# Attention softmax in whole-tile operations: subtraction and row sum on VectorE, one exponential a chunk on ScalarE

## The chip, the cores and the metric

The kernel runs on one core of a Trainium2 chip. A core has five engines that work side by side and are ordered by semaphores: TensorE (PE, matrix products into PSUM), VectorE (DVE), ScalarE (ACT), GpSimd (POOL) and SyncE (SP, which here only starts transfers). Each engine works through its own instructions in order. The metric is the device time of one execution in microseconds; the time given is the median of several executions.

## The reference

One layer of a hybrid encoder over 1024 frames of 1024 channels, float32. A projection feeds three token mixers (gated DeltaNet, RWKV-7, sliding-window attention with sinks), whose outputs are gated, summed, projected and normalised; a feed-forward part follows. The change is in the attention branch. Frames come in 16 chunks of 64; a chunk's 64 queries read the 128 keys of the chunk before and their own, for 8 heads. What is computed there:

```python
s = einsum(qc, kb) * SD ** -0.5 - slope * dist      # [8 heads, 64 queries, 128 keys] a chunk
s = where(key_chunk >= 0, s, -inf)
p = softmax(concatenate([s, sink], -1), axis=-1)[..., :-1]
o = einsum(p, vb)
```

The sink is one learned logit per head that takes part in the maximum and in the sum, and has no value of its own.

## The kernel before, in words

The program is a row of stages, each with its own block of instructions for every engine: the projection and the preparation of operands; `scan_and_attend` (L1054), which runs both recurrences over the 16 chunks and does the attention in between; `mix_and_project`; `feed_forward`. A stage starts when the one before has ended on all engines, its last stores included. The change is in `scan_and_attend` alone.

The order of the work there is written out by hand. Each engine has three generators for a chunk: `product(c)` (products of a chunk's operands that don't need the state), `state(c)` (what needs the recurrent state and updates it) and `attend(c)`. `run` (L1110) takes their parts in turn by the list `TURNS`: in the loop of chunk c these are `state(c)`, `product(c + 1)` and `attend(c)`. Every engine follows the same list, so that one engine's queue fixes what stands behind a waiting instruction.

The attention of a chunk holds its 8 x 64 rows of scores as one tile `score[b]` of 128 partitions x (4 x 128) columns, two tiles in turn. Four numbers belong to each partition: `top` (maximum), `own` (the sink's part) and `rest` (the sum), tiles of 128x4. PE computes the scores (L1278). On DVE follow the scaling with the ALiBi penalty (L1364), the row maximum (L1366), the maximum with the sink (L1368), sink minus maximum (L1370) and the maximum's sign turned (L1371). ACT takes the exponential of `own` (L1431) and four exponentials of 128x128, each with the negative maximum as bias and the row sum as accumulated output (L1433). In a later turn DVE adds the sink's part to the sum (L1374), takes the reciprocal (L1376) and multiplies the tile by it (L1378). PE transposes the weights (L1285), ACT copies them out of PSUM (L1437), PE multiplies them with the values (L1293), ACT copies the result out (L1442).

In DVE's order around this: after the maximum's part come `state`'s sums of the new state, L1339 (waits for PE's L1243), L1342 (`s_g`) and L1349 (`sv`), then `product`'s L1323 (`zt`), then L1374 to L1378; the next chunk's L1329 and L1333 (`r_tmp`, `r_g`), L1313, L1316, L1318 follow, and then L1364 again. In ACT's order L1433 is followed by L1420 (waits for PE's L1204) and L1411 (waits for PE's L1264). POOL, once DVE has finished `s_g`, scales it (L1482, `s_dec`), copies inverse blocks (two L1466, four L1470) and scales `tok_g` (L1473), then waits for the next `s_g`; it runs one chunk ahead, so that its copies end before the last two chunks.

Of the kernel before, what the change touches and what calls it, by code (L numbers as in the profile page):

```python
# [18 lines left out]
ALU = mybir.AluOpType  # L19
ACT = mybir.ActivationFunctionType  # L20
AX = mybir.AxisListType

P = 128
# [97 lines left out]
class Phase(ExitStack):  # L121
# [7 lines left out]
    def sem(self, name):  # L129
        self.sems.append(self.held.enter_context(self.nc.semaphore(name)))  # L130
        return self.sems[-1]
# [918 lines left out]
def rwkv_rows(e):  # L1050
    return slice(64 * e, 64 * e + 64)


def scan_and_attend(nc, home, opnd, xinv, gates_tile, cols, egl_bc, plast, mixed, u, attended, par, tab, const_dram):  # L1054
# [8 lines left out]
    with Phase(nc, home) as local:  # L1063
# [20 lines left out]
        W = 2 * C  # L1084
        keys, values = (local.enter_context(nc.sbuf_tensor(n, shape, F32)) for n, shape in (("at_keys", [P, SKV, C + T]), ("at_values", [P, C + T])))
        alibi = local.enter_context(nc.sbuf_tensor("at_alibi", [P, 8 * W], F32))
        score, weight, vt = two("at_score", [4, W]), local.enter_context(nc.sbuf_tensor("at_weight", [P, 4, W], F32)), two("at_vt", [P])
        top, own, rest = two("at_top", [4]), two("at_own", [4]), two("at_rest", [4])
# [11 lines left out]
        mm_sc, mm_t, mm_pv, vt_done, scored, topped, exp_done, rested, p_done, weight_done, at_done = (  # L1100
            sem("at_" + n) for n in ("mm_sc", "mm_t", "mm_pv", "vt_done", "scored", "topped", "exp_done", "rested", "p_done", "weight_done", "done"))
# [8 lines left out]
        def run(product, state, attend):  # L1110


            first = product(0)
            for _ in range(4):
                next(first, None)
            for c in range(NCH):
                parts = {"state": state(c), "product": product(c + 1) if c + 1 < NCH else iter(()), "attend": attend(c)}
                for part in TURNS:
                    next(parts[part], None)
# [182 lines left out]
        @block.vector  # L1302
        def _(dve):
            for e in range(2):
                dve.memset(sv[0][rwkv_rows(e), of(e), :], 0.0).then_inc(s_rw_done, 1)
            dve.memset(s_g[0][:, :, :], 0.0).then_inc(s_g_done, 2)

            def product(c):
                b, d = c % 2, c % DEEP
                dve.wait_ge(mm_m, c + 1)  # L1310
                for e in range(2):
                    other = rwkv_rows(1 - e)
                    dve.tensor_tensor(ar[d][other, of(e), 0, :], ps_m[e][other, :, 0, :], bc("strict", 4, other), ALU.mult).then_inc(masked, 1)  # L1313
                yield
                for e in range(2):
                    dve.tensor_tensor(causal[b][:, of(e), :], ps_m[e][:, :, 1, :], bc("causal", 4), ALU.mult).then_inc(masked, 1)  # L1316
                dve.wait_ge(mm_a, c + 1)
                dve.tensor_tensor(attn[b][:, :, :], ps_a[:, 0:2, :],  # L1318
                                  gates_tile[:, c:c + 1, :, 1, :].rearrange("p o g s -> p (o g) s"), ALU.mult).then_inc(attn_done, 1)
                yield  # L1320
                dve.wait_ge(mm_z, c + 1)
                dve.wait_ge(inv_done, c * 4 + 4)
                dve.tensor_tensor(zt[b][:, :, :], ps_z, inv[b][:, 1, :, :], ALU.add).then_inc(zt_done, 1)  # L1323
                yield

            def state(c):
                b, d = c % 2, c % DEEP
                dve.wait_ge(mm_r, c + 1)
                dve.tensor_tensor(r_tmp[b][:, :, :], ps_r[:, 256:512].rearrange("p (g d) -> p g d", g=2),  # L1329
                                  cols[:, c:c + 1, 2, :].rearrange("p o g -> p (o g)").unsqueeze(2).to_broadcast([P, 2, GD]), ALU.mult).then_inc(r_tmp_done, 1)  # L1330
                dve.wait_ge(r_tmp_done, c + 1)
                dve.wait_ge(tok_done, c + 1)
                dve.tensor_tensor(r_g[b][:, :, :], r_tmp[b][:, :, :], tok_g[b][:, 1, :, :], ALU.add).then_inc(r_g_done, 1)  # L1333
                yield
                yield
                dve.wait_ge(mm_s, c + 1)
                for e in range(2):
                    h = rwkv_rows(e)
                    dve.tensor_tensor(s_sum[b][h, :, :], sv[d][h, of(e), :], ps_r[h, 0:256].rearrange("p (j d) -> p j d", j=4), ALU.add).then_inc(s_sum_done, 1)  # L1339
                dve.wait_ge(dec_done, c + 1)  # L1340
                for e, src in enumerate((ps_w[:, 0:256], ps_r[:, 256:512])):
                    last = dve.tensor_tensor(s_g[1 - b][:, :, :].rearrange("p (g e) d -> p g e d", e=2)[:, :, e, :],  # L1342
                                             s_dec[b][:, :, :].rearrange("p (g e) d -> p g e d", e=2)[:, :, e, :],
                                             src.rearrange("p (g d) -> p g d", g=2), ALU.add)
                    last.then_inc(s_g_done, 1)
                dve.wait_ge(s_sum_done, c * 2 + 2)
                for e in range(2):
                    h = rwkv_rows(e)
                    dve.tensor_tensor(sv[(c + 1) % DEEP][h, of(e), :], s_sum[b][h, :, :],  # L1349
                                      plast[h, :].rearrange("p (j c) -> p j c", j=4)[:, :, c:c + 1].to_broadcast([64, 4, C]), ALU.mult).then_inc(s_rw_done, 1)  # L1350
                yield

            def attend(c):
                b = c % 2
                at = 4 * W if c == 0 else 0
                flat = lambda x: x.rearrange("p j k -> p (j k)")
                yield
                yield
                if c == 0:
                    dve.wait_ge(alibi_landed, 16)  # L1360
                dve.wait_ge(mm_sc, c + 1)
                if c >= 2:
                    dve.wait_ge(mm_t, c - 1)
                dve.scalar_tensor_tensor(flat(score[b][:, :, :]), ps_at[:, :], SD ** -0.5, alibi[:, at:at + 4 * W], ALU.mult, ALU.add).then_inc(scored, 1)  # L1364
                dve.wait_ge(scored, c + 1)
                dve.tensor_reduce(top[b][:, :], score[b][:, :, :], AX.X, ALU.max).then_inc(topped, 1)  # L1366
                dve.wait_ge(topped, 4 * c + 1)
                dve.tensor_tensor(top[b][:, :], top[b][:, :], par("sinks", 0, 4), ALU.max).then_inc(topped, 1)  # L1368
                dve.wait_ge(topped, 4 * c + 2)
                dve.tensor_tensor(own[b][:, :], par("sinks", 0, 4), top[b][:, :], ALU.subtract).then_inc(topped, 1)  # L1370
                dve.tensor_scalar(top[b][:, :], top[b][:, :], -1.0, None, ALU.mult).then_inc(topped, 1)  # L1371
                yield
                dve.wait_ge(exp_done, 5 * c + 5)
                dve.tensor_tensor(rest[b][:, :], rest[b][:, :], own[b][:, :], ALU.add).then_inc(rested, 1)  # L1374
                dve.wait_ge(rested, 2 * c + 1)
                dve.reciprocal(rest[b][:, :], rest[b][:, :]).then_inc(rested, 1)  # L1376
                dve.wait_ge(rested, 2 * c + 2)
                dve.tensor_tensor(score[b][:, :, :], score[b][:, :, :], rest[b][:, :].unsqueeze(2).to_broadcast([P, 4, W]), ALU.mult).then_inc(p_done, 1)  # L1378
                yield
                yield  # L1380

            run(product, state, attend)

        @block.scalar
        def _(act):
# [38 lines left out]
            def attend(c):  # L1424
                b = c % 2
                if c:
                    store_attended(c - 1)
                yield
                yield
                act.wait_ge(topped, 4 * c + 4)  # L1430
                act.activation(own[b][:, :], own[b][:, :], ACT.Exp).then_inc(exp_done, 1)  # L1431
                for j in range(4):
                    act.activation(score[b][:, j, :], score[b][:, j, :], ACT.Exp, bias=top[b][:, j:j + 1], accum_out=rest[b][:, j:j + 1]).then_inc(exp_done, 1)  # L1433
                yield
                yield
                act.wait_ge(mm_t, c + 1)
                act.activation(weight[:, :, :], at_t, ACT.Copy).then_inc(weight_done, 1)  # L1437
                yield

            def store_attended(c):  # L1440
                act.wait_ge(mm_pv, c + 1)
                act.activation(attended[:, :, c * C:(c + 1) * C], ps_at[:, 0:4 * C].rearrange("p (j s) -> p j s", j=4), ACT.Copy).then_inc(at_done, 1)  # L1442

            run(product, state, attend)
            store_attended(NCH - 1)
            finish(NCH - 1)
# [804 lines left out]
```

## Time and profile before

| | us |
|---|---|
| median of 3 runs | 2146.53 (2145.28 to 2147.59) |
| the profiled execution's own time | 2144.27 |
| its span, first to last instruction | 2142.4 |
| PE busy in the span | 1976.5 (92%) |
| DVE busy | 1100.6 (51%) |
| ACT busy | 581.8 (27%) |
| POOL busy | 564.3 (26%) |

The busy shares are means over all stages. The stage of the change is the stretch from about 855 to 1076 us. Busy times of several engines overlap. A row of a timeline gives start and duration in us, then engine, line, operation and tiles; in brackets stands how long the engine had been idle before and what it waited for.

### The profile page before, as it was taken

To read this page: it belongs to the slowest core of one execution; us is meant where nothing else is said; L and a number is where in the kernel's file an instruction comes from. 1 tells how busy PE (TensorE), PEld (TensorE's weight loads), DVE (VectorE), ACT (ScalarE), POOL (GpSimd) and SP (SyncE) were. 2 spreads that over 40 slices of the span, in tenths; PEclk is the share of its full clock that TensorE was granted. 3 is DMA by queue.
4 is the path that set the end of the run, shared out by engine and by line. 5 is a ranking of instruction groups with operands and counts; after the bars stand their busy time and mean duration, and the time that the engine had idled before them with its cause. 6 is when DMAs were issued, how large, how long until landed. Compare 5 with 4: busy or idle time off the path is not lost. (4 is left out here: it accounts for less than half of the span.)

```text
span 2142.4 us, 28824 instructions
## 1 busy us (share of the span) xinstructions
PE 1976.5 (92%) x11456; PEld 1575.0 (74%) x11456; DVE 1100.6 (51%) x1351; ACT 581.8 (27%) x926; POOL 564.3 (26%) x357
## 2 busy tenths in 40 slices
PE   5998889999999997999888899599999999999995
PEld 4876668767788885777666678488888888888884
DVE  3666764566449600666668744522433434424337
ACT  2443423235321211444442221212212112121112
POOL 3211111211122322434242372422212122122113
PEclk9999989999999998999999999799999999999998
DMA  5243565135753554666364460211111111111101
GB/s 141 52 80 93 130 153 147 40 89 134 177 148 97 127 124 127 188 187 193 90 187 144 135 207 20 59 60 59 49 39 59 29 59 59 29 59 44 44 20 79
DMA packets 340405, 211.83 MB, mean 99 GB/s; under 512 B 170796, under 2 KB 310700, under 8 KB 338256
## 3 DMA queue, kind: packets, MB, share of 16 engines
q1 hardware_dynamic: 264112, 156.33, 27.4%
q10 hardware_dynamic: 75568, 54.04, 8.8%
q8 instruction: 71, 1.16, 0.2%
q0 software_dynamic: 624, 0.05, 0.1%
q14 instruction: 30, 0.25, 0.0%
HBM read 151.27 MB, written 59.06 MB: 98 GB/s over the span
## 5 line engine op out<-in xcount | busy, mean ns | idle before, releaser
L154 PE MATMUL bank<-xhi,w_hi 128*128 128x512 f32 x976 | 396.3, 406 | 2.9 <-DVE xlo L868 2.9
L155 PE MATMUL bank<-xlo,w_hi 128*128 128x512 f32 x976 | 387.8, 397 | 0.0
L156 PE MATMUL bank<-xhi,w_lo 128*128 128x512 f32 x976 | 387.1, 397 | 0.0
L394 POOL TENSOR_TENSOR w_lo<-w_raw,w_hi 128x1024 fp32r<-128x1024 f32 x61 | 163.0, 2673 | 640.5 <-ACT w_hi L731 640.5
L2139 DVE TENSOR_TENSOR ff_hid<-ff_hid,ff_ps_u 128x512 f32<-128x512 f32 x42 | 28.9, 687 | 416.8 <-PE ff_ps_u L156 416.8
L154 PEld LDWEIGHTS bank<-xhi,w_hi 128*128 128x128 f32 x976 | 185.0, 190 | 49.1 <-issue 3.5
L156 PEld LDWEIGHTS bank<-xhi,w_lo 128*128 128x128 f32 x976 | 184.7, 189 | 44.9
L155 PEld LDWEIGHTS bank<-xlo,w_hi 128*128 128x128 f32 x976 | 184.9, 189 | 44.7 <-issue 2.4
L2147 DVE TENSOR_TENSOR y<-y,ff_d 128x512 f32<-128x512 f32 x320 | 199.0, 682 | 0.0
L2050 POOL TENSOR_TENSOR ff_lo_down<-ff_raw_down,ff_hi_down 128x1024 fp32r<-128x1024 f32 x22 | 52.9, 2405 | 533.0 <-ACT ff_hi_down L1987 533.0
L154 PE MATMUL ff_ps_g<-x1hi,ff_hi_gate 128*128 128x512 f32 x352 | 137.8, 391 | 18.2 <-POOL ff_lo_gate L2050 18.2
L154 PE MATMUL ff_d<-ff_hi_down,ff_hhi 128*128 128x512 f32 x352 | 139.8, 397 | 4.8 <-DVE ff_hlo L2156 3.9
L155 PE MATMUL ff_d<-ff_lo_down,ff_hhi 128*128 128x512 f32 x352 | 138.1, 392 | 0.0
L156 PE MATMUL ff_d<-ff_hi_down,ff_hlo 128*128 128x512 f32 x352 | 138.1, 392 | 0.0
L155 PE MATMUL ff_ps_g<-x1lo,ff_hi_gate 128*128 128x512 f32 x352 | 137.4, 390 | 0.0
L156 PE MATMUL ff_ps_g<-x1hi,ff_lo_gate 128*128 128x512 f32 x352 | 137.4, 390 | 0.0
L154 PE MATMUL ff_ps_u<-x1hi,ff_hi_up 128*128 128x512 f32 x352 | 136.9, 389 | 0.0
L155 PE MATMUL ff_ps_u<-x1lo,ff_hi_up 128*128 128x512 f32 x352 | 136.9, 389 | 0.0
L156 PE MATMUL ff_ps_u<-x1hi,ff_lo_up 128*128 128x512 f32 x352 | 136.9, 389 | 0.0
L717 ACT ACTIVATE work<-bank 128x512 f32<-128x512 f32 x70 | 41.9, 598 | 274.5 <-PE bank L156 269.4
L154 PEld LDWEIGHTS ff_ps_g<-x1hi,ff_hi_gate 128*128 128x128 f32 x352 | 66.5, 189 | 32.4 <-POOL ff_lo_gate L2050 18.6
L154 PEld LDWEIGHTS ff_d<-ff_hi_down,ff_hhi 128*128 128x128 f32 x352 | 66.5, 189 | 27.7 <-DVE y L2147 9.4
(320 smaller groups left out, 3527.4 us busy)
## 6 DMA issues: line engine op xcount, KB each, us to landing
w_raw<-in_w_in ACTq DMA_DIRECT2D x61, 512.0 KB, 4.2
op<-opnd SPq DMA_DIRECT2D x16, 1152.0 KB, 5.6
u<-work ACTq DMA_DIRECT2D x68, 256.0 KB, 3.4
b_gate<-u SPq DMA_DIRECT2D x24, 512.0 KB, 3.8
ff_raw_gate<-in_ffn_gate SPq DMA_DIRECT2D x22, 512.0 KB, 4.0
ff_raw_up<-in_ffn_up SPq DMA_DIRECT2D x22, 512.0 KB, 5.3
ff_raw_down<-in_ffn_down SPq DMA_DIRECT2D x22, 512.0 KB, 5.8
opnd<-work SPq DMA_DIRECT2D x20, 512.0 KB, 6.2
```

What stands on the lines that cost most here:

```text
L154: pe.matmul(out, w_hi, x_hi, start=first, stop=False)
L155: pe.matmul(out, w_hi, x_lo, start=False, stop=False)
L156: return pe.matmul(out, w_lo, x_hi, start=False, stop=last)
L394: pool.tensor_tensor(w_lo[b][:, :, :], w_raw[b][:, :, :], as_f32(w_hi[b][:, :, :]), ALU.subtract).then_inc(w_lo_done, 1)
L717: act.activation(to, bank[(done_at[q] - 1) % 3][:, :], form(tile)).then_inc(evac, 1)
L2050: pool.tensor_tensor(wlo[b][n][:, :, :], raw[b][n][:, :, :], as_f32(whi[b][n][:, :, :]), ALU.subtract).then_inc(lo_done, 1)
L2139: dve.tensor_tensor(hid[:, h, :], hid[:, h, :], ps_u[:, h, :], ALU.mult).then_inc(mul_done, 1)
L2147: dve.tensor_tensor(part, part, ps_d[n % 4][:, :], ALU.add).then_inc(added, 1)
```

## The change

Before the exponential DVE subtracts the maximum from the whole 128x512 tile, with the maximum broadcast along each row, in place of turning the maximum's sign. ACT takes one exponential over the tile, without a bias and without the accumulated sums, in place of four. After it DVE sums the rows with a reduction over the tile, in front of the addition of the sink's part. The semaphore counts follow: two signals a chunk from ACT in place of five, three steps in place of two for `rested`. The maximum's part still signals `topped` four times.

```diff
--- before.py
+++ after.py
@@ -1368,13 +1368,15 @@
                 dve.tensor_tensor(top[b][:, :], top[b][:, :], par("sinks", 0, 4), ALU.max).then_inc(topped, 1)
                 dve.wait_ge(topped, 4 * c + 2)
                 dve.tensor_tensor(own[b][:, :], par("sinks", 0, 4), top[b][:, :], ALU.subtract).then_inc(topped, 1)
-                dve.tensor_scalar(top[b][:, :], top[b][:, :], -1.0, None, ALU.mult).then_inc(topped, 1)
-                yield
-                dve.wait_ge(exp_done, 5 * c + 5)
+                dve.tensor_tensor(score[b][:, :, :], score[b][:, :, :], top[b][:, :].unsqueeze(2).to_broadcast([P, 4, W]), ALU.subtract).then_inc(topped, 1)
+                yield
+                dve.wait_ge(exp_done, 2 * c + 2)
+                dve.tensor_reduce(rest[b][:, :], score[b][:, :, :], AX.X, ALU.add).then_inc(rested, 1)
+                dve.wait_ge(rested, 3 * c + 1)
                 dve.tensor_tensor(rest[b][:, :], rest[b][:, :], own[b][:, :], ALU.add).then_inc(rested, 1)
-                dve.wait_ge(rested, 2 * c + 1)
+                dve.wait_ge(rested, 3 * c + 2)
                 dve.reciprocal(rest[b][:, :], rest[b][:, :]).then_inc(rested, 1)
-                dve.wait_ge(rested, 2 * c + 2)
+                dve.wait_ge(rested, 3 * c + 3)
                 dve.tensor_tensor(score[b][:, :, :], score[b][:, :, :], rest[b][:, :].unsqueeze(2).to_broadcast([P, 4, W]), ALU.mult).then_inc(p_done, 1)
                 yield
                 yield
@@ -1429,8 +1431,7 @@
                 yield
                 act.wait_ge(topped, 4 * c + 4)
                 act.activation(own[b][:, :], own[b][:, :], ACT.Exp).then_inc(exp_done, 1)
-                for j in range(4):
-                    act.activation(score[b][:, j, :], score[b][:, j, :], ACT.Exp, bias=top[b][:, j:j + 1], accum_out=rest[b][:, j:j + 1]).then_inc(exp_done, 1)
+                act.activation(score[b][:, :, :], score[b][:, :, :], ACT.Exp).then_inc(exp_done, 1)
                 yield
                 yield
                 act.wait_ge(mm_t, c + 1)
```

## Rows read from the trace of the kernel before

**Rows 1.** Stretch, length; busy us (count) of PE, PEld, DVE, ACT, POOL; clock; DMA.

```profile
945.00:958.15 13.15, 12.48 (x224) 9.94 (x224) 9.13 (x23) 5.52 (x21) 5.19 (x8) 1.00 0.59 171
...
1050.00:1063.00 13.00, 10.48 (x186) 8.14 (x184) 7.66 (x20) 5.70 (x21) 1.09 (x1) 1.00 0.08 24
```

**Rows 2.** Waits from 868 to 1063 us: us in total, times, longest.

```profile
DVE s_sum L1339 <- PE ps_r L1243: 21.2, 15, 1.6
...
PE ps_at L1285 <- DVE at_score L1378: 6.9, 14, 0.7
```

**Rows 3.** Timeline of DVE around chunk 6: start us, us, line, tiles.

```profile
944.97 0.87 DVE L1339 TENSOR_TENSOR s_sum<-sv,ps_r 64x256 f32<-64x256 f32 x2 [1.40 <-PE ps_r L1243]
...
946.53 1.60 DVE L1349 TENSOR_TENSOR sv<-s_sum,plast 64x256 f32<-64x256 f32 x2
...
946.97 1.16 DVE L1349 TENSOR_TENSOR sv<-s_sum,plast 64x256 f32<-64x256 f32 x1
...
948.17 0.56 DVE L1323 TENSOR_TENSOR zt<-ps_yz,inv 128x384 f32<-128x384 f32 x1
...
948.64 0.15 DVE L1374 TENSOR_TENSOR at_rest<-at_rest,at_own 128x4 f32<-128x4 f32 x1
...
949.04 0.80 DVE L1378 TENSOR_TENSOR at_score<-at_score,at_rest 128x512 f32<-128x512 f32 x1
...
955.55 0.69 DVE L1366 TENSOR_REDUCE at_top<-at_score 128x4 f32<-128x512 f32 x1
...
956.55 0.16 DVE L1371 TENSOR_SCALAR at_top<-at_top 128x4 f32<-128x4 f32 x1
...
958.11 0.87 DVE L1339 TENSOR_TENSOR s_sum<-sv,ps_r 64x256 f32<-64x256 f32 x2 [1.40 <-PE ps_r L1243]
```

**Rows 4.** Timeline of ACT in the same chunk.

```profile
956.98 0.27 ACT L1393 ACTIVATE at_vt<-ps_yz 128x128 f32<-128x128 f32 x1
...
957.23 0.40 ACT L1433 ACTIVATE at_score<-at_score,at_top 128x128 f32<-128x128 f32 x1
...
958.77 0.37 ACT L1420 ACTIVATE o<-ps_a 128x256 f32<-128x256 f32 x1
...
962.61 0.38 ACT L1411 ACTIVATE o_tok<-ps_o 128x256 f32<-128x256 f32 x1 [3.47 <-PE ps_o L1264]
```

**Rows 5.** Timeline of PE in the same chunk.

```profile
949.90 0.66 PE L1285 MATMUL ps_at<-tables,at_score 128*128 128x128 f32 x4 [0.48 <-DVE at_score L1378]
...
957.99 0.44 PE L1204 MATMUL ps_a<-tables,o_tok 128*128 128x128 f32 x2
```

**Rows 6.** Timeline of POOL in the same chunk.

```profile
946.76 1.09 POOL L1482 TENSOR_TENSOR s_dec<-s_g,egl_bc 128x512 f32<-128x512 f32 x1 [7.45 <-DVE s_g L1342]
...
948.80 0.50 POOL L1470 COPY inv<-inv_packed 32x384 f32<-32x384 f32 x1
...
949.36 0.85 POOL L1470 COPY inv<-inv_packed 32x384 f32<-32x384 f32 x1
```

**Rows 7.** Timeline of DVE and POOL in chunk 7.

```profile
959.68 0.86 DVE L1349 TENSOR_TENSOR sv<-s_sum,plast 64x256 f32<-64x256 f32 x2
...
961.05 0.42 DVE L1374 TENSOR_TENSOR at_rest<-at_rest,at_own 128x4 f32<-128x4 f32 x1
...
961.72 0.75 DVE L1378 TENSOR_TENSOR at_score<-at_score,at_rest 128x512 f32<-128x512 f32 x1
...
960.19 1.26 POOL L1482 TENSOR_TENSOR s_dec<-s_g,egl_bc 128x512 f32<-128x512 f32 x1 [7.74 <-DVE s_g L1342]
...
961.59 0.33 POOL L1466 COPY join<-inv_corner 32x192 f32<-32x192 f32 x1
```

**Rows 8.** Timeline of DVE and PE in chunk 15, the last.

```profile
1064.96 0.69 DVE L1378 TENSOR_TENSOR at_score<-at_score,at_rest 128x512 f32<-128x512 f32 x1
...
1065.77 0.66 PE L1285 MATMUL ps_at<-tables,at_score 128*128 128x128 f32 x4
```

**Rows 9.** Line L1437: durations ns min/median/max, first and last start, form.

```profile
L1437 ACT ACTIVATE at_weight<-ps_at x16: 597/597/597, 871.7 to 1066.5; 128x512 f32<-128x512 f32 x16
```

## The prediction

> **What bounds the kernel now.** The change touches only the stage that scans the chunks and attends, so I read the stretch from about 855 to 1076 us and took the rest as it is. First the busy times of one ordinary chunk [rows 1]: PE works 12.48 of 13.15 us at a granted clock of 1.00, DVE 9.13, ACT 5.52, POOL 5.19. PE works through its instructions in order, so the question is what its few gaps wait for. The table of waits [rows 2] answers it: PE stands before the transposes of the weights (L1285) in 14 chunks, 6.9 us in all, for DVE's last multiplication (L1378). DVE in its turn waits 21.2 us over 15 chunks for the products behind L1243. That closes the loop that makes the chunk's length. The timeline of chunk 6, counted from 0, shows it: DVE starts L1339 at 944.97, runs without a pause up to the end of L1378 at 949.84, PE starts L1285 at 949.90, and PE's work from there leads to L1339 of the next chunk at 958.11 [rows 3, 5]. 4.93 us of DVE and handover plus 8.21 us led by PE make the period of 13.14. Whatever makes DVE's run from L1339 to L1378 longer makes every chunk longer. Work elsewhere costs nothing while its cover lasts.
>
> **The maximum's half of the change** (before the exponential). The 128x4 multiplication by -1 (0.16 us) goes, and a 128x512 subtraction with a broadcast operand comes. It has the shape of L1378: 0.69 us alone, 0.80 beside POOL [rows 3, 8]. It starts at 956.55, where POOL stands idle (7.74 us before its s_dec in chunk 7) [rows 7], so I take 0.69 and end at 957.24. DVE then waits anyway until 958.11, 1.40 us behind the present last instruction [rows 3]. The cost of 0.53 (0.64 with the contended duration) is hidden, and 0.87 of cover remain. It counts only if that wait vanishes.
>
> **ScalarE.** Four exponentials with their accumulator reads now run from 957.23 to 958.77, 1.54 us [rows 4]. One over 128x512 replaces them. The nearest row is the 0.60 us copy of that size from PSUM [rows 9]; even the bounds, one 128-wide exponential (0.40) and the present 1.54, lead to the same answer. It waits for the subtraction, so the small exponential in front starts at about 957.3 instead of 957.14 and the large one ends near 958.0. Behind it in ACT's queue stands L1420, which needs PE's L1204, ended at 958.43, so it starts 0.3 us sooner and ACT then idles 3.8 us instead of 3.47 for L1411 [rows 4, 5]. DVE's first reader of the sums starts at 961.05 [rows 7], 3 us after that end (2.3 after the present one). ScalarE's saving of some 0.9 us a chunk is therefore worth nothing.
> The Trainium skill, "VectorE: DVE Perf Modes", section on the TRN2 errata, gives ScalarE a fixed extra latency per instruction that large tiles amortise, which argues for this merge. The trace agrees on the size (0.40 for 128 columns, 0.60 for 512); summed at face value over 16 chunks it would promise 15 us, of which I count none, since no wait of rows 2 ends on ACT's exponential.
>
> **The sum's half** (after the exponential). A reduction of 128x512 comes before the small addition. The same form takes 0.69 us at L1366, with 0.036 to the next dependent instruction [rows 3]: +0.72, all of it inside DVE's run to L1378. Nothing covers it. This is the first term.
>
> **The second term is POOL.** The added reduction moves the last three operations to another place beside POOL's copies, and the rows show that the two engines take turns. The second L1349 starts at 946.97 and should take 0.41; it takes 1.16 and ends 0.28 after POOL's s_dec has ended (946.76 + 1.09 = 947.85). L1378 starts at 949.04 in the first inv copy, which ends at 949.30, and ends 0.54 after it. The second copy, started at 949.36, takes 0.85 in place of 0.50 and ends 0.37 after L1378. In chunk 7 even the 4-column L1374 takes 0.42 and ends with s_dec at 961.47 [rows 3, 6, 7]. L1323 and L1339, with one operand in PSUM, do not show it. So a DVE instruction with two SBUF inputs stands until a POOL instruction that got in first has ended, and the other way round.
> New order: the reduction, one input, runs from 948.64 to about 949.33; the first copy is over at 949.30; the addition starts at 949.35 or 949.36, together with the second copy at 949.36. Who gets in first? A stopped instruction has its beginning behind it by then: the second copy 0.13 us (its 0.50 less the 0.37 that followed L1378), a DVE instruction 0.13 (L1349: 0.41 less 0.28) to 0.15 (L1378: 0.69 less 0.54). By this the copy gets in at 949.49 and the addition between 949.48 and 949.51. I choose the copy, knowing that it is close.
> Then the addition ends 0.02 behind the copy, at 949.88. The multiplication starts 0.25 later, as now (948.79 to 949.04, with the reciprocal between), at 950.13, inside the third copy (949.92 to 950.42), and ends 0.54 behind that, at 950.96, where it was 949.84: +1.12 a chunk. If the addition gets in first, it ends at 949.51, and the multiplication starts at 949.76, finds the second copy just over and ends at 950.45: +0.61, counted as 0.62.
> The Trainium skill, "SBUF — State Buffer", section "Who interferes with whom", says that GpSimd and a VectorE instruction with two SBUF inputs contend, that whoever issues first keeps the shared ports for the whole instruction, and that a reduction never contends. The rows agree (1.16 for 0.41; L1366 is always 0.69, though POOL is idle beside it, so the reduction's part is not shown here).
>
> **Sum.** POOL copies run in chunks 0 to 13. In chunk 14 POOL has one instruction left, s_dec (1.09 us from 1050 to 1063) [rows 1], so it pays 0.72. In chunk 15 PE starts L1285 at 1065.77 without a wait on DVE, 0.12 behind the end of L1378 at 1065.65, where 0.06 is the usual handover (949.84 to 949.90), so 0.66 of the 0.72 arrive [rows 3, 5, 8]. 14 x 1.12 + 0.72 + 0.66 = 17.1 us. The next stage begins behind this one's last stores, so the shift is passed on. The profiled execution took 2144.27 us (span 2142.4), so 2161.4 in its terms; the median of the runs shown is 2.3 above it, and 2146.5 + 17.1 gives 2163.6. I write 2163.5.
>
> **Rivals.**
> A. The addition gets in first. 14 x 0.62 + 0.72 + 0.66 = 10.1 us, 2156.6. For it: the margin is as small as the rounding of the rows. Against it: the order worked out above.
> B. Not slower. In chunk 7, POOL's s_dec starts 0.51 us after the first L1349 (959.68, 960.19) instead of 0.23 (946.53, 946.76), so that the second L1349 gets in first and the pair takes 0.86 in place of 1.60; that chunk's run from L1339 (958.11) to the end of L1378 (962.47) is 4.36 instead of 4.87 [rows 3, 6, 7]. If the new timing gave every chunk this order, then: reduction 961.05 to 961.73, addition behind the first join copy (961.59 + 0.33) to 961.96, multiplication (started at 962.21) behind the second (961.98 to 962.33) to 962.87, so 4.76: 0.11 below today's ordinary chunk. 13 x -0.11, chunk 7 itself +0.40, and 1.38 for the last two give +0.4: 2146.9, no change. It decides when s_dec starts more than about 0.2 us later than it does in 14 of 15 chunks. Against it: the change touches nothing between s_g and s_dec.
> C. ScalarE's saving lies on the path. Even then a chunk has -0.94 + 0.53 + 0.72 = +0.31, 5 us over 16 chunks: 2151.5. Against it: the 3 us between its end and its reader.
> D. The reduction is held up by POOL as well, or holds up a copy into which the addition then runs: up to one copy's remainder, some 0.35 us a chunk on top of the forecast, 14 x 0.35 = 5: 2168.5.
> The clock is not among them: in the chunk with the largest gaps PE worked 10.48 of 13 us and was still granted 1.00 [rows 1], and the new chunk has 12.5 of 14.3.
>
> **How the numbers follow.** Forecast 0.50, A 0.33, B 0.08, C 0.03, D 0.04, something else with a gain 0.02. The range reaches from A with its error of the median (2154.5) to short of D (2167). Between no change and either sign this kernel's runs tell 0.2%, 4.3 us. Forecast, A, C and D are slower: 0.90. B is no change: 0.08. Faster: 0.02.
>
> **What would show it.** Right: the period of an ordinary chunk goes from 13.15 to about 14.27 us; the small addition takes about 0.5 instead of 0.15; PE's wait before L1285 grows from 0.48 to 1.6; DVE's wait at L1339 falls from 1.40 to about 0.9; ACT's wait before L1411 grows to 3.8; the new exponential takes about 0.6. With A, the addition takes 0.15 and the period is 13.77. With B the pair at L1349 takes 0.86 in most chunks. Wrong altogether: a period that stays, or a wait before L1285 that ends on ACT; also a granted clock below 1.00 inside the stage, which would make it slower than the range.

## The result and the profile after

| | before | changed |
|---|---|---|
| median, us | 2145.91 (2143.68 to 2147.59, 4 runs) | 2158.38 (2154.70 to 2158.89, 4 runs) |
| profiled execution, us | 2144.27 | 2154.70 |
| its span, us | 2142.4 | 2152.9 |
| period of an ordinary chunk, us | 13.15 | 13.75 |

The changed kernel is slower by a factor of 1.0055, 95% interval 1.0038 to 1.0072; 12.5 us between the medians, 10.4 us between the two profiled executions. The direction and the range were right. The forecast case (+1.12 us a chunk) was not the one that came: rival A did, in which VectorE's small addition gets in ahead of POOL's second copy.

DVE of the changed kernel in chunk 6, the answer to [rows 3]. L1371 is now the subtraction, L1374 the added reduction, L1376 the addition, L1380 the multiplication:

```profile
948.70 0.68 DVE L1371 TENSOR_TENSOR at_score<-at_score,at_top 128x512 f32<-128x512 f32 x1
950.26 0.87 DVE L1339 TENSOR_TENSOR s_sum<-sv,ps_r 64x256 f32<-64x256 f32 x2 [0.88 <-PE ps_r L1243]
...
951.83 1.60 DVE L1349 TENSOR_TENSOR sv<-s_sum,plast 64x256 f32<-64x256 f32 x2
953.46 0.56 DVE L1323 TENSOR_TENSOR zt<-ps_yz,inv 128x384 f32<-128x384 f32 x1
953.93 0.68 DVE L1374 TENSOR_REDUCE at_rest<-at_score 128x4 f32<-128x512 f32 x1
954.64 0.16 DVE L1376 TENSOR_TENSOR at_rest<-at_rest,at_own 128x4 f32<-128x4 f32 x1
954.84 0.18 DVE L1378 RECIPROCAL at_rest<-at_rest 128x4 f32<-128x4 f32 x1
955.05 0.69 DVE L1380 TENSOR_TENSOR at_score<-at_score,at_rest 128x512 f32<-128x512 f32 x1
...
964.01 0.87 DVE L1339 TENSOR_TENSOR s_sum<-sv,ps_r 64x256 f32<-64x256 f32 x2 [0.88 <-PE ps_r L1243]
```

The run from L1339 to the end of the multiplication is 950.26 to 955.74, 5.48 us, where it was 4.87. The reduction brings 0.71 with its handover, and the multiplication gives 0.11 back, 0.69 for 0.80 (the sum, 0.60, and the 0.61 of the runs differ by rounding). From one L1339 to the next it is 13.75. In the maximum's half the subtraction (0.68) takes its time out of DVE's wait, 0.88 instead of 1.40.

ACT and PE in the same chunk, the answer to [rows 4, 5]:

```profile
949.52 0.61 ACT L1434 ACTIVATE at_score<-at_score 128x512 f32<-128x512 f32 x1
950.61 0.38 ACT L1422 ACTIVATE o<-ps_a 128x256 f32<-128x256 f32 x1 [0.48 <-PE ps_a L1204]
...
954.75 0.38 ACT L1413 ACTIVATE o_tok<-ps_o 128x256 f32<-128x256 f32 x1 [3.75 <-PE ps_o L1264]
```

```profile
955.80 0.66 PE L1285 MATMUL ps_at<-tables,at_score 128*128 128x128 f32 x4 [1.09 <-DVE at_score L1380]
```

The one exponential takes 0.61 us where four took 1.54. Of the 0.93 us saved, ACT waits 0.76: 0.48 in front of L1422, where it had no wait, and 3.75 in front of L1413 for 3.47. The rest goes in front of its exponentials, which start later behind the subtraction. PE's wait before the transposes is 1.09 for 0.48; that 0.61 is the loss of a chunk.

POOL's copies beside them, the answer to [rows 6]:

```profile
954.09 0.50 POOL L1471 COPY inv<-inv_packed 32x384 f32<-32x384 f32 x1
...
954.64 0.54 POOL L1471 COPY inv<-inv_packed 32x384 f32<-32x384 f32 x1
...
955.24 0.87 POOL L1471 COPY inv<-inv_packed 32x384 f32<-32x384 f32 x1
```

The addition and the second copy start at the same printed 954.64. The addition keeps its 0.16 and the copy takes 0.54, so the addition went first. The first copy runs beside the reduction and keeps its 0.50, and the reduction keeps its 0.68: a reduction, with one input, does not take turns with POOL here. The prediction had no row for it; this is one. The Trainium skill, "SBUF — State Buffer", section "Who interferes with whom", says the same, that a reduction never contends with GpSimd.

The first and the last L1339 of both profiles tell how much of the 10.4 us is the stage's (durations in ns, then first and last start in us). Kernel before, then changed kernel:

```profile
L1339 DVE TENSOR_TENSOR s_sum<-sv,ps_r x32: 411/420/426, 866.1 to 1062.5; 64x256 f32<-64x256 f32 x32
```

```profile
L1339 DVE TENSOR_TENSOR s_sum<-sv,ps_r x32: 411/419/426, 867.7 to 1073.2; 64x256 f32<-64x256 f32 x32
```

Before, the distance is 196.4 us, after 205.5, which is +9.0 before rounding, and +0.65 behind it up to the start of the next stage (1071.17 and 1082.49 for its first ACT instruction). That is 9.7 us of the stage: 13 chunks of 0.61, chunk 7 with 0.41, chunk 14 with 0.72, and the end. The changed kernel's stage began 1.7 us later, which is the execution and not the change, and the later stages took 0.8 us less. The difference of the medians, 12.5, has the same noise in it.

### The profile page after: what moved, and what is told of

Read it like the earlier page. It is cut to its first block and busy times, and to the rows that moved or that the text cites. A ratio compares the mean times of both kernels' runs of the same rounds, so it can differ in the third digit from the quotient of the medians.

```text
span 2152.9 us, 28728 instructions
## 1 busy us (share of the span) xinstructions
PE 1979.3 (92%) x11456; PEld 1576.7 (73%) x11456; DVE 1116.5 (52%) x1367; ACT 568.5 (26%) x814; POOL 564.8 (26%) x357
## 3 DMA queue, kind: packets, MB, share of 16 engines
q8 instruction: 71, 1.16, 0.2%
```

## The experiments

The theory, called P in the expectations, is that of the prediction: only VectorE's run from L1339 to the multiplication sets the length of a chunk, and in that run VectorE takes turns with POOL. Q and S let every VectorE or ScalarE microsecond count. The experiments ran in two sets, each on one chip together with the kernel before: x1 to x4 (its median there 2146.76 over 23 runs) and x5 to x8 (2146.17 over 17). Every ratio is to the kernel before of the same set.

**x1_max_half.** The subtraction alone.

```diff
-                dve.tensor_scalar(top[b][:, :], top[b][:, :], -1.0, None, ALU.mult).then_inc(topped, 1)
+                dve.tensor_tensor(score[b][:, :, :], score[b][:, :, :], top[b][:, :].unsqueeze(2).to_broadcast([P, 4, W]), ALU.subtract).then_inc(topped, 1)
...
-                    act.activation(score[b][:, j, :], score[b][:, j, :], ACT.Exp, bias=top[b][:, j:j + 1], accum_out=rest[b][:, j:j + 1]).then_inc(exp_done, 1)
+                    act.activation(score[b][:, j, :], score[b][:, j, :], ACT.Exp, accum_out=rest[b][:, j:j + 1]).then_inc(exp_done, 1)
```

> Only the maximum's half: VectorE subtracts the maximum from the tile (L1371 as in the changed kernel), ScalarE keeps four exponentials with accumulated sums, without a bias; nothing is added after them. Theory P (only VectorE's run from L1339 to the last multiplication sets the chunk): time as before within 2 us, period of a chunk 13.15, VectorE's wait at L1339 falls from 1.40 to about 0.88. Theory Q (each added VectorE microsecond counts): 16 x 0.53 = 8.5 us slower.

Measured: 2145.55 us, ratio 0.9997 (0.9984 to 1.0010).

```profile
943.03 0.68 DVE L1371 TENSOR_TENSOR at_score<-at_score,at_top 128x512 f32<-128x512 f32 x1
944.59 0.87 DVE L1339 TENSOR_TENSOR s_sum<-sv,ps_r 64x256 f32<-64x256 f32 x2 [0.88 <-PE ps_r L1243]
...
948.67 0.80 DVE L1378 TENSOR_TENSOR at_score<-at_score,at_rest 128x512 f32<-128x512 f32 x1
...
957.74 0.87 DVE L1339 TENSOR_TENSOR s_sum<-sv,ps_r 64x256 f32<-64x256 f32 x2 [0.88 <-PE ps_r L1243]
```

The period is 13.15 as before (once 13.29) and the wait 0.88. The subtraction is free; Q's 8.5 us lie outside the interval.

**x2_sum_half.** The reduction alone: four exponentials with bias, without `accum_out`, and the changed kernel's reduction with its counts.

```diff
-                    act.activation(score[b][:, j, :], score[b][:, j, :], ACT.Exp, bias=top[b][:, j:j + 1], accum_out=rest[b][:, j:j + 1]).then_inc(exp_done, 1)
+                    act.activation(score[b][:, j, :], score[b][:, j, :], ACT.Exp, bias=top[b][:, j:j + 1]).then_inc(exp_done, 1)
...
+                dve.tensor_reduce(rest[b][:, :], score[b][:, :, :], AX.X, ALU.add).then_inc(rested, 1)
```

> Only the sum's half: ScalarE takes four exponentials with the bias but without the accumulated sums, VectorE reduces the tile before the small addition. Theory P: as slow as the changed kernel, 10 us over the kernel before, period 13.75 (+0.61), last multiplication 0.69 instead of 0.80, PE's wait before the transposes 1.09. Theory Q: less than the changed kernel by the subtraction's 8.5 us, so about 4 us over before.

Measured: 2158.77 us, ratio 1.0054 (1.0036 to 1.0073). The whole loss of the change is here. Its trace shows more: the small addition took 0.16 us in most chunks, and 0.51 in four. Two neighbours, chunks 5 and 6: DVE, then PE's wait, then POOL's second copy of each:

```profile
944.60 0.16 DVE L1376 TENSOR_TENSOR at_rest<-at_rest,at_own 128x4 f32<-128x4 f32 x1
...
958.35 0.51 DVE L1376 TENSOR_TENSOR at_rest<-at_rest,at_own 128x4 f32<-128x4 f32 x1
...
959.10 0.84 DVE L1380 TENSOR_TENSOR at_score<-at_score,at_rest 128x512 f32<-128x512 f32 x1
```

```profile
945.75 0.66 PE L1285 MATMUL ps_at<-tables,at_score 128*128 128x128 f32 x4 [1.09 <-DVE at_score L1380]
...
960.00 0.66 PE L1285 MATMUL ps_at<-tables,at_score 128*128 128x128 f32 x4 [1.59 <-DVE at_score L1380]
```

```profile
944.59 0.53 POOL L1472 COPY inv<-inv_packed 32x384 f32<-32x384 f32 x1
...
958.34 0.50 POOL L1472 COPY inv<-inv_packed 32x384 f32<-32x384 f32 x1
```

Both times the copy starts 0.01 us before the addition; once the addition passes (the copy takes 0.53), once it stands (0.51) and the multiplication then stands behind the third copy (0.84). The forecast case and rival A occur side by side in one execution, and PE's wait is then 1.59, the forecast's 1.6. The trace holds whole nanoseconds, and these part the cases: in the nine chunks where the addition passed it had started 0 to 4 ns after the copy, in the four where it stood 5 or 6 ns after it. In the changed kernel's profile it lies between 1 ns before and 4 ns after, and always passes.

From the first to the last L1339 x2 takes 210.7 us in its profile, 5.2 more than the changed kernel: 4 x 0.50 for these chunks and two periods that are longer by 1.6 us each (see x7). The medians (2158.77 and 2158.38) are nearly equal all the same. Whether the changed kernel has such chunks in its other executions, which lie 3.5 to 4.2 us above the profiled one, no trace shows.

**x3_one_exp.** ScalarE's merge alone.

```diff
-                for j in range(4):
-                    act.activation(score[b][:, j, :], score[b][:, j, :], ACT.Exp, bias=top[b][:, j:j + 1], accum_out=rest[b][:, j:j + 1]).then_inc(exp_done, 1)
+                act.activation(score[b][:, :, :], score[b][:, :, :], ACT.Exp).then_inc(exp_done, 1)
```

The kernel leaves out the subtraction of the maximum and the row sums: `rest` is filled with ones at the start (two lines more, so that later line numbers of DVE are higher by 2), and DVE waits for two signals of ACT in place of five.

> Only ScalarE's merge: one exponential over the tile in place of four; the maximum is not subtracted and the row sums are not formed (left out), VectorE's instructions are those of the kernel before. Theory P: no change within 2 us although ScalarE has about 0.9 us a chunk less to do; ScalarE's wait for PE's L1264 grows by that. Theory S (ScalarE's time counts): up to 15 us faster.

Measured: 2145.47 us, ratio 0.9995 (0.9983 to 1.0007); periods of 13.15 again (once 13.33). ScalarE's waits before L1420 and L1411 (L1422 and L1413 here) take up what it saves, 0.60 and 0.28 us of the 0.91:

```profile
948.33 0.63 ACT L1434 ACTIVATE at_score<-at_score 128x512 f32<-128x512 f32 x1
949.56 0.38 ACT L1422 ACTIVATE o<-ps_a 128x256 f32<-128x256 f32 x1 [0.60 <-PE ps_a L1204]
...
953.70 0.38 ACT L1413 ACTIVATE o_tok<-ps_o 128x256 f32<-128x256 f32 x1 [3.75 <-PE ps_o L1264]
```

The merge brings nothing here, in either direction. The profiled execution, 2149.97 us, is above that median: in its last chunk PE ran at a granted clock of 0.50 (same columns as in [rows 1]), where the kernel before had 1.00:

```profile
1067.00:1075.00 8.00, 7.31 (x57) 4.56 (x56) 2.74 (x8) 1.44 (x5) 0.00 (x0) 0.50 0.09 33
```

**x4_later.** The changed kernel with the run's last four instructions pushed back a little.

```diff
+                dve.tensor_reduce(top[b][:, 0:1], top[b][:, :], AX.X, ALU.max)
                 dve.tensor_reduce(rest[b][:, :], score[b][:, :, :], AX.X, ALU.add).then_inc(rested, 1)
```

> The changed kernel with one more reduction over 4 columns (result not used) in front of the row sum, so that the row sum, the addition, the reciprocal and the multiplication move by about 0.08 us against POOL. Theory P with turn taking between VectorE and POOL: the small addition now meets POOL's second inv copy after that copy has got in, takes about 0.5 instead of 0.16, and the multiplication stands behind the third copy; period about 14.3 instead of 13.75, some 7 us slower than the changed kernel. Rival, no such edge (the place beside the copies doesn't matter): period 13.83, 1.3 us slower.

Measured: 2170.03 us, ratio 1.0102 (1.0078 to 1.0126), 11.65 us above the changed kernel's median, more than either expectation.

```profile
936.16 0.15 DVE L1374 TENSOR_REDUCE at_top<-at_top 128x1 f32<-128x4 f32 x1
936.23 0.68 DVE L1375 TENSOR_REDUCE at_rest<-at_score 128x4 f32<-128x512 f32 x1
936.94 0.45 DVE L1377 TENSOR_TENSOR at_rest<-at_rest,at_own 128x4 f32<-128x4 f32 x1
...
937.64 0.84 DVE L1381 TENSOR_TENSOR at_score<-at_score,at_rest 128x512 f32<-128x512 f32 x1
```

```profile
936.88 0.50 POOL L1472 COPY inv<-inv_packed 32x384 f32<-32x384 f32 x1
```

With the addition 0.06 us behind the copy it stands in 13 of 14 chunks (all but chunk 7, whose s_dec is late in this kernel too), and the ordinary period is 14.26: the forecast case, almost to the hundredth (14.27). From the first to the last L1339 the stage took 218.5 us in this profile, 13.0 more than the changed kernel's. The forecast case explains 6.7 of it, 13 x 0.51 and a little at the end. The other 6.3 are in four chunks that took 15.84, 1.58 more than the rest. (The profiled execution, 2175.67, is the slowest of x4's four; 8 of the 21 us by which it exceeds the changed kernel's lie outside the stage.) Windows over an ordinary chunk, over the next, and over one more of the four (PE, PEld, DVE, ACT, POOL busy, granted clock, DMA share, GB/s):

```profile
902.38:916.65 14.27, 12.48 (x224) 9.94 (x225) 10.54 (x25) 4.74 (x13) 5.18 (x8) 1.00 0.53 157
916.65:932.49 15.84, 14.05 (x224) 11.35 (x225) 10.53 (x25) 4.85 (x13) 5.18 (x8) 0.89 0.69 194
961.00:976.84 15.84, 14.06 (x224) 11.35 (x225) 10.53 (x25) 4.85 (x13) 5.18 (x8) 0.89 0.49 142
```

The 5.3 us behind PE's wait, in the ordinary chunk and in the slow one after it:

```profile
908.43:913.73 5.30, 5.30 (x100) 4.77 (x100) 2.83 (x8) 1.26 (x3) 1.36 (x2) 1.00 0.97 302
922.70:928.00 5.30, 5.30 (x64) 4.61 (x66) 1.28 (x3) 1.37 (x3) 1.35 (x2) 0.68 0.97 303
```

PE stood from 921.10 to 922.70 for the multiplication, and the chunk's 224 matmuls took 14.05 us instead of 12.48. Right behind the wait the granted clock was 0.68 over 5.3 us, a mixture of the two levels (1.2 and 2.4 GHz), and 64 matmuls ran where the chunk before had 100. The transfers do not tell the two apart: their share is 0.97 in this stretch either way, and over the whole chunk 0.53 in an ordinary one, 0.69 and 0.49 in slow ones. But the ordinary chunk has the same wait of 1.60 us, so whether the wait is the cause is still open; x7 tests it.

**x7_later_filled.** x4_later with PE kept busy in that wait.

```diff
+                pe.wait_ge(scored, c + 1)
+                for j in range(10):
+                    pe.transpose(at_t[:, j % 4, :], tab("ident"), tab("ident"))
                 pe.wait_ge(p_done, c + 1)
```

> The kernel x4_later (PE waits 1.6 us before the transposes of each chunk, and four chunks of its profile took 15.84 instead of 14.25 us at a granted clock of 0.89), with ten transposes of a constant tile in PE's queue in front of that wait, overwritten by the real ones: some 1.2 of the 1.6 us are filled, nothing waits for them. If PE's idle stretch is what lets the clock fall: granted clock 1.00 in every chunk, all periods 14.25, some 6 us faster than x4_later although PE has more to do. If the slow chunks come from a transfer or another engine: they stay at 15.84.

Measured: 2162.29 us, ratio 1.0075 (1.0060 to 1.0090), 7.7 us below x4_later. In its trace every ordinary chunk takes 14.26 us and none 15.84, with PE's useful work and VectorE's blocked addition (0.45) as they were. PE's wait is left at 0.36, and behind it the clock stays at 1.00 beside the same transfers:

```profile
918.88:924.18 5.30, 5.30 (x100) 4.77 (x100) 2.84 (x8) 1.25 (x3) 1.36 (x2) 1.00 0.98 304
```

The two intervals overlap a little, so it is the periods that carry this, in one profile of each kernel: the slow chunks come with PE's idle stretch, not with the transfers. In x2 two of the 15 periods are longer by 1.6 us in the same way, at 0.89 and behind waits of 1.47 and 1.59 us, while three other waits of 1.59 us there cost nothing.

**x8_after_filled.** The changed kernel with six such transposes (`range(6)`).

> The changed kernel with six such transposes in front of the same wait (0.8 of 1.09 us filled). Its profiled execution showed no chunk at a lower clock, but its other runs lie 3.5 to 4 us above that one. If some executions have two or three chunks of 15.3 us at the lower clock: runs at about 2154.5, 3 to 4 us below the changed kernel's median. If not: same as the changed kernel, or slower if the added transposes reach past VectorE's multiplication.

Measured: 2157.72 us, ratio 1.0049 (1.0036 to 1.0062), no different from the changed kernel. The stage took nearly the same time (first to last of these sums, L1339 there and L1342 here, 205.7 us for 205.5), and of the 3.7 us by which its profiled execution (2158.40) exceeds that of the changed kernel, 3.5 lie in the stages behind. Filling the wait of 1.09 us gained nothing, which agrees with the granted clock of 1.00 that the changed kernel has behind it. The expectation's guess found no support: in x8 the higher time is not the clock in this stage. What makes the later stages vary by 3 to 4 us stays open.

**x5_pool_waits_before.** The kernel before, with POOL kept out of VectorE's run.

```diff
                 pool.wait_ge(s_g_done, c * 2 + 2)
+                if c:
+                    pool.wait_ge(p_done, c)
                 pool.tensor_tensor(s_dec[b][:, :, :], s_g[b][:, :, :], egl_bc[:, :, c:c + 1].to_broadcast([P, GH, GD]), ALU.mult).then_inc(dec_done, 1)
```

> The kernel before, with one wait more: POOL starts s_dec only after VectorE's last multiplication of the chunk, so that its 5.2 us of work no longer stand beside VectorE's run from L1339 to that multiplication. Turn taking between the two engines as the cause of the 1.60 us pair at L1349: the pair takes 0.86, the multiplication 0.69, PE's wait before the transposes (0.48) goes, period 12.65 instead of 13.15, 7 us faster than before. If the 1.60 has another cause: no change.

Measured: 2138.13 us, ratio 0.9965 (0.9952 to 0.9978), faster than both kernels.

```profile
942.26 0.87 DVE L1339 TENSOR_TENSOR s_sum<-sv,ps_r 64x256 f32<-64x256 f32 x2 [1.40 <-PE ps_r L1243]
...
943.83 0.86 DVE L1349 TENSOR_TENSOR sv<-s_sum,plast 64x256 f32<-64x256 f32 x2
...
945.60 0.69 DVE L1378 TENSOR_TENSOR at_score<-at_score,at_rest 128x512 f32<-128x512 f32 x1
```

```profile
946.64 0.66 PE L1285 MATMUL ps_at<-tables,at_score 128*128 128x128 f32 x4
```

```profile
946.46 1.05 POOL L1484 TENSOR_TENSOR s_dec<-s_g,egl_bc 128x512 f32<-128x512 f32 x1 [7.16 <-DVE at_score L1378]
```

```profile
942.26:954.86 12.60, 12.41 (x224) 9.94 (x225) 8.08 (x23) 5.44 (x21) 4.92 (x8) 1.00 0.61 178
```

The pair at L1349 takes 0.86, the multiplication 0.69 and POOL's own s_dec 1.05; PE no longer waits before the transposes and the period is 12.60. VectorE's run from L1339 to the end of the multiplication (942.26 to 946.29) is shorter by 0.84 us, 4.03 for 4.87, and the period only by 0.55: with its wait gone PE is busy 12.41 of 12.60 us (the window above), and the run no longer sets the length of the chunk. A wait added to one engine made the kernel 8 us faster.

**x6_pool_waits_after.** The changed kernel with the same two lines.

> The changed kernel with the same wait for POOL. Turn taking as the cause: VectorE's run is 0.74 shorter, PE's wait before the transposes falls from 1.09 to about 0.35, period about 13.0 instead of 13.75, 10 to 11 us faster than the changed kernel and about 1 to 2 us below the kernel before. Otherwise: no change against the changed kernel.

Measured: 2144.33 us, ratio 0.9992 (0.9984 to 1.0001) to the kernel before. PE's wait is left at 0.36 and the period is 13.02:

```profile
953.02 0.66 PE L1285 MATMUL ps_at<-tables,at_score 128*128 128x128 f32 x4 [0.36 <-DVE at_score L1380]
```

The periods give 10 to 11 us against the changed kernel, as expected (first to last L1339 195.3 for 205.5); the medians give 14, over two sets. That x6 is below the kernel before, as expected, is not shown: the interval holds 1. The reduction still costs 0.42 a chunk against x5, so x5 is the best version.

## Why the prediction was right, and where not

- What bounds the chunk: right. x1 and x3 add and remove work outside VectorE's run and change nothing; x2 and x6 change the run, and the period follows. In x5 it follows until PE's wait is used up.
- The maximum's half: right. 0.68 instead of the 0.69 taken, hidden, with 0.88 of the wait left (0.87 forecast), and x1 shows it alone.
- ScalarE: right. 0.61 for the 0.60 of the nearest row (a copy out of PSUM, so that the closeness of the two is partly luck), ACT's wait 3.75 for the 3.8 forecast, and x3 shows that the saving is worth nothing.
- The sum's half, first term: right. +0.71 forecast as 0.72, not covered; x2 alone is as slow as the whole change.
- The second term, POOL: the mechanism was right, the size wrong. "I choose the copy, knowing that it is close" failed: the addition got in first in 13 of the 14 chunks that have copies, so such a chunk cost 0.61 and not 1.12. In chunk 7, where s_dec is late, the addition started 0.6 us before the first inv copy and met none of them; that chunk cost 0.41, which the sum had at 1.12 and rival B at 0.40. This is the term mis-sized in the sum: 14 x 1.12 = 15.7 us, where the trace has 13 x 0.61 + 0.41 = 8.3. The whole stage came to 9.7 us for the 17.1 of the sum and the 10.1 of rival A. x2 shows why no reading of the rows could settle it: with starts printed 0.01 us apart the order falls either way in one execution, for a difference of nanoseconds, and x4 shows that 0.06 us more decides it. A forecast there should have been given by the two cases with nearly the same chance.
- Rival A's sum was close, one of its steps was wrong: "finds the second copy just over". By the prediction's own 0.37 that copy ends at 949.88, after the multiplication's start at 949.76, and so it was: the multiplication started at 955.05, the copy ended at 955.18. It took its 0.69 all the same, which fits the prediction's own reading that some 0.15 us of a multiplication pass before it can be stopped.
- The claim that the clock is not among the rivals held for the changed kernel, whose PE waits 1.09 us. It did not hold for the forecast case itself: with waits of 1.6 us or more four chunks of x4 lost 1.58 us each. "The chunk with the largest gaps" before (1050 to 1063 us) had its idle time in three gaps, of 0.37, 0.87 and 1.28 us, and its 1.00 said nothing about one longer stretch. x4 has the run of the forecast case and took 2170.03 us, outside the stated range. That the range held is therefore partly luck: it held because rival A came.
- Rival B's mechanism, a late s_dec, was seen only in chunk 7, as before; x5 shows what it is worth when it is brought about on purpose. Rivals C and D are ruled out, C by x3 and D by the reduction's 0.68 and the 0.50 of the copy beside it.

## What to carry to other kernels

Merging instructions on an engine gains nothing while the bounding one does not wait for it; here the merge also moved the row sums from an engine that idled to the one run that nothing covered. In such a run list each VectorE instruction with two SBUF inputs against what POOL does at that moment, since here the two took turns and a shift of 0.06 us cost 0.5 us a pass; where POOL's work has time, make it wait until the run is over. A price that hangs on who starts first within the rounding of the trace is to be forecast as two cases.

## What was not expected of the hardware

- A stopped VectorE instruction or POOL copy stands until the other has ended whole: even a 128x4 addition took 0.45 to 0.51 us in place of 0.16, one 256-column multiplication 1.16 in place of 0.41, and a POOL copy 0.85 in place of 0.50. The order was settled within nanoseconds: in x2 an addition that started up to 4 ns after the copy passed, and one that started 5 or 6 ns after it stood.
- PE's granted clock fell after single idle stretches of 1.5 to 2.0 us, though PE was busy 12.5 of 14.3 us around them: to 0.89 over the period (0.68 over 5.3 us of one), in 4 of the 15 periods of x4; the same in 2 of x2. It fell in none of x7, where the stretch was filled, and in none of the changed kernel, whose waits before the transposes reach 1.15 us at most. Shorter stretches may cost it too: PE stands 1.28 us before L1238 in chunk 14 of every kernel, and in x3's profile alone the clock was at 0.50 after it, from 1067 to 1075 us, while the others kept 1.00 through the last chunk. Why some of these waits are followed by a lower clock and others not is left open.
- In chunk 7 of every kernel s_dec began some 0.28 us late, whatever the time of that chunk was. Where POOL waits for the multiplication (x5) it is late as well (idle 7.46 us instead of 7.16) and nothing follows from it. The cause was not looked for.
